# A two-layer mixer and expert step: one expert's up weights go to another place and are loaded before the scatters end, and a VectorE copy moves ahead of a register load

## The reference

```
def moe_ffn(h, w_router, b_router, w1, w3, w2):
    s = jax.nn.sigmoid((h @ w_router).astype(jnp.float32))
    sb = s + b_router.astype(jnp.float32)
    ...
    _, idx = lax.top_k(jnp.where(in_group, sb, NEG_INF), TOP_K)
    wsel = jnp.take_along_axis(s, idx, axis=-1)
    wsel = wsel / jnp.sum(wsel, axis=-1, keepdims=True)
    gates = ...
    hid = jax.nn.silu(jnp.einsum('bnd,edf->bnef', h, w1)) * jnp.einsum('bnd,edf->bnef', h, w3)
    return jnp.einsum('bnef,efd->bnd', hid * gates[..., None], w2).astype(h.dtype)
```

## Time and profile before

| what | value |
|---|---|
| median of 3 runs | 1187.36 us (1186.56 to 1190.74) |
| the profiled execution's own time | 1180.08 us |
| its span, first to last instruction | 1177.2 us |
| mean granted TensorE clock | 0.978 |
| busy share of the span: PE, PE weight loads, VectorE, ScalarE, GpSimd | 93%, 48%, 44%, 23%, 18% |
| chain that ended last: PE, DMA, VectorE, GpSimd | 74%, 11%, 5%, 4% |
| bytes moved by DMA | 288.29 MB, mean 245 GB/s |

### The profile page before, as it was taken

How to read it: one execution, slowest core, us unless ns; L and a number is a source line. 1 busy time by engine, 2 the same in 40 slices (tenths; PEclk the granted TensorE clock), 3 DMA queues, 4 the chain that set the end, 5 groups by cost and what they waited for, 6 DMA issues and landing times.

```text
span 1177.2 us, 14999 instructions
## 1 busy us (share of the span) xinstructions
PE 1094.7 (93%) x5084; PEld 569.2 (48%) x5084; DVE 522.6 (44%) x1291; ACT 275.8 (23%) x637; POOL 212.2 (18%) x297
## 2 busy tenths in 40 slices
PE   5999999899999799999899999989999988899985
PEld 3556766555444343345345576655544433234432
DVE  1133554776236542424351535478623563224236
ACT  2121121566011111111152112156601111111111
POOL 5027100101122310000363510010112231000022
PEclk9999899999999899999999999999999978999998
DMA  9587741795404899998565841179300489999834
GB/s 348 212 273 279 277 179 36 292 355 213 179 0 170 335 376 365 417 417 355 208 259 187 345 168 66 36 272 360 120 18 1 154 325 348 368 417 414 333 131 189
DMA packets 62842, 288.29 MB, mean 245 GB/s; under 512 B 9776, under 2 KB 10944, under 8 KB 46832
## 3 DMA queue, kind: packets, MB, share of 16 engines
q1 hardware_dynamic: 33344, 190.87, 42.4%
q0 software_dynamic: 22608, 77.70, 18.4%
q10 hardware_dynamic: 6816, 18.78, 4.2%
HBM read 237.96 MB, written 55.93 MB: 250 GB/s over the span
## 4 chain that ended last, share of the span: by engine, by line
PE 74%; DMA 11%; DVE 5%; POOL 4%; issue 3%; ACT 2%; SPq 1%; another core or an unknown queue 0%; ACTq 0%; POOLq 0%; DVEq 0%
PE ps L1797 14%; PE ps L1319 12%; PE ps L1620 12%; PE ps L1821 6%; DMA arena<-in_w 5%; PE ps L1554 3%; PE ps L1585 2%; PE ps L1254 2%; PE ps L1247 2%; PE ps L1565 2%; DMA bias_rows<-bias_tab 2%; PE ps L1855 1%; PE ps L1185 1%; DVE arena L2659 1%; PE ps L1230 1%
## 5 line engine op out<-in xcount | busy, mean ns | idle before, releaser
L1797 PE MATMUL ps<-arena 128*32 128x512 f32 (+1 forms) x1024 | 206.0, 616 | 10.5 <-DMA arena<-in_w 9.6
L1319 PE MATMUL ps<-arena 128*128 128x320 f32 x560 | 159.7, 439 | 2.9 <-DVE arena L2426 2.9
L1620 PE MATMUL ps<-arena 128*128 128x512 f32 x320 | 140.4, 594 | 2.4 <-issue 2.4
L1797 PEld LDWEIGHTS ps<-arena 128*32 128x32 f32 (+1 forms) x1024 | 74.7, 134 | 136.6 <-issue 135.1
L1319 PEld LDWEIGHTS ps<-arena 128*128 128x128 f32 x560 | 106.7, 193 | 47.0 <-DVE arena L2426 3.1
L2924 DVE COPY arena<-ps 128x512 f32<-128x512 f32 x28 | 19.4, 691 | 193.4 <-PE ps L1761 193.4
L1821 PE MATMUL ps<-arena 128*32 128x512 f32 (+1 forms) x512 | 101.6, 595 | 3.3 <-issue 3.3
L1620 PEld LDWEIGHTS ps<-arena 128*128 128x128 f32 x320 | 59.5, 190 | 74.6 <-issue 74.6
L1131 POOL DMA_DIRECT2D arena<-expert_in x36 | 18.8, 521 | 262.5 <-issue 262.5
L1821 PEld LDWEIGHTS ps<-arena 128*32 128x32 f32 (+1 forms) x512 | 34.3, 129 | 50.6 <-issue 50.6
L2169 ACT ACTIVATE arena<-ps 128x256 f32<-128x256 f32 x28 | 10.7, 383 | 186.9 <-PE ps L1797 186.9
(11 more groups left out here) (349 smaller groups left out, 1570.8 us busy)
## 6 DMA issues: line engine op xcount, KB each, us to landing
arena<-in_w SPq DMA_DIRECT2D x96, 1024.0 KB, 17.4
arena<-in_w_ada SPq DMA_DIRECT2D x40, 1024.0 KB, 6.9
expert_in<-arena POOLq DMA_DIRECT2D x2, 8192.0 KB, 32.1
arena<-in_w_t SPq DMA_DIRECT2D x10, 1024.0 KB, 10.0
arena<-in_w_ada_c SPq DMA_DIRECT2D x8, 1024.0 KB, 13.2
arena<-in_w_out SPq DMA_DIRECT2D x8, 1024.0 KB, 7.4
arena<-mod_rows POOLq DMA_DIRECT2D x16, 512.0 KB, 11.4
arena<-in_w_n SPq DMA_DIRECT2D x8, 928.0 KB, 9.3
```

The lines of the kernel that those rows point to most:

```text
L1319: ins = mm(out[:, 0:HALF], lhs[:, k, :], rhs[:, k, :], start=(first and k == 0), stop=(last and k == 3), skip_group_check=True)
L1620: ins = mm(out[:, n * 512:(n + 1) * 512], yT[:, k, t * P:(t + 1) * P], w[k // 2][:, k % 2, n * 512:(n + 1) * 512], start=(k == 0), stop=(k ...
L1797: ins = mm(out[lo:lo + n, :], hsT[b][:, k, lo:lo + n], w[role][:, k, :], start=(k == 0), stop=(k == KD - 1), skip_group_check=True)
```

## The change

Four things change, in both layers.

1. Place 2's up weights (role 2 is the first in it) go to `at_y`, columns 0 to 4095, in place of `at_h + 2 * SLOT`. Place 2's down weights are cut in two pieces of 1024 columns, the last 1024 columns of `at_h` and the last 1024 of `at_y`; sizes and the count of DMAs stay.
2. SyncE issues the two DMAs of up 2 after `roles_ready` alone. The waits for `tokens0` and for the scatters come after them, ahead of up 5.
3. VectorE's copy of the upper half of `tokens0` comes ahead of `value_load(rounds_i)`.
4. Six VectorE instructions that find role and capacity of each token's choices and the last unit's gates move from ahead of the loop to `rows_of_round`, which lies behind the copy of unit 0's transposed tokens. Their products go to an own buffer `r_chosen`, and their waits use another semaphore.

```
-        up_at = [at_ring + SLOT, at_ring + 3 * SLOT, at_h + 2 * SLOT, at_h]
-        down_at = [at_ring, at_ring + 5 * SLOT, at_h + 4 * SLOT, at_up]
+        up_at = [at_ring + SLOT, at_ring + 3 * SLOT, at_y, at_h]
+        down_home = [view(at_ring, 2, D), view(at_ring + 5 * SLOT, 2, D), view(at_h + TL * D, 2, KD * N_TOK)[:, :, 0:D], view(at_up, 2, D)]
...
+        r_chosen = view(at_a + D, 2, TT, NE)
...
                     wait(sp, roles_ready.sem, roles_ready.at(l, 1))
-                    filled(sp, l, "tokens0")
-                    wait(sp, scattered.sem, scattered.at(l, 16 * 2 * TT))
...
-                        for load, role in WEIGHTS_ORDER:
+                        for n, (load, role) in enumerate(WEIGHTS_ORDER):
+                            if n == 1:
+                                filled(sp, l, "tokens0")
+                                wait(sp, scattered.sem, scattered.at(l, 16 * 2 * TT))
...
-                for of_expert, of_choice in ((r_role_row, r_role), (r_cap_of, r_cap)):
-                    link(V(r_t, r_sel, of_expert.unsqueeze(1).unsqueeze(1).broadcast_to((P, 2, TT, NE)), ALU.mult))
-                    link(dve.tensor_reduce(of_choice, r_t, AX.X, ALU.add))
                 if l + 1 < DEPTH:
                     modulation_rows(l, l + 1)
                     modulation_columns(l, l + 1)
                     gates_of_choices()
-                link(dve.scalar_tensor_tensor(out=r_gate2, in0=r_role, scalar=float((NE - 1) * P), in1=gates,
-                                              op0=ALU.is_equal, op1=ALU.mult))
-                link(V(r_gate, r_gate2[:, 0], r_gate2[:, 1], ALU.add))
...
                 def rows_of_round(turn):
+                    for n, (of_expert, of_choice) in enumerate(((r_role_row, r_role), (r_cap_of, r_cap))):
+                        V(r_chosen, r_sel, of_expert.unsqueeze(1).unsqueeze(1).broadcast_to((P, 2, TT, NE)), ALU.mult)\
+                            .then_inc(back_chain, 1)
+                        dve.wait_ge(back_chain, turn * 16 + (2 * n + 1))
+                        dve.tensor_reduce(of_choice, r_chosen, AX.X, ALU.add).then_inc(back_chain, 1)
+                        dve.wait_ge(back_chain, turn * 16 + (2 * n + 2))
...
                 dve.sem_inc(passed, 1)
+                dve.tensor_copy(hs[:, 0, 512:1024], filled(dve, l, "tokens0")[:, 512:1024]).then_inc(first_high.sem, 1)
                 n_rounds = dve.value_load(rounds_i[0:1, 0:1], min_val=1, max_val=5)
-                dve.tensor_copy(hs[:, 0, 512:1024], filled(dve, l, "tokens0")[:, 512:1024]).then_inc(first_high.sem, 1)
```

More of the change, by code:

```diff
@@ L35 @@
 CREDIT = 2
-DVE_CHAIN = 171
+DVE_CHAIN = 165
 ROUNDS = N_TOK // P
@@ L859, in load_down @@
                     wait(sp, dn_full, used_down)
-                    sp.dma_start(view(down_at[q], 2, D), A["w2"][bass.ds(l, 1), bass.ds(e, 1), :, :]
+                    sp.dma_start(down_home[q], A["w2"][bass.ds(l, 1), bass.ds(e, 1), :, :]
                                  .rearrange("a b (k p) n -> p (a b k) n", p=P)).then_inc(down_in[q][0], 16)
@@ L1812, in down @@
                     for role, _, _, _ in EXPERT_UNITS[u]:
-                        w[role] = view(down_at[loaded(down_in, turn, role, 16)], 2, D)
+                        w[role] = down_home[loaded(down_in, turn, role, 16)]
                     pe.wait_ge(hidT_ready, base + u + 1)
@@ L2947, in rows_of_round @@
                 def rows_of_round(turn):
+                    for n, (of_expert, of_choice) in enumerate(((r_role_row, r_role), (r_cap_of, r_cap))):
[4 more added lines that the diff above has]
+                        dve.wait_ge(back_chain, turn * 16 + (2 * n + 2))
+                    dve.scalar_tensor_tensor(out=r_gate2, in0=r_role, scalar=float((NE - 1) * P), in1=gates,
+                                             op0=ALU.is_equal, op1=ALU.mult).then_inc(back_chain, 1)
+                    dve.wait_ge(back_chain, turn * 16 + 5)
+                    V(r_gate, r_gate2[:, 0], r_gate2[:, 1], ALU.add).then_inc(back_chain, 1)
                     role = r_role.rearrange("p a t -> p (a t)")
@@ L2954, in rows_of_round @@
                     dve.tensor_scalar(r_last, r_rel2, 1.0, None, ALU.add).then_inc(back_chain, 1)
-                    dve.wait_ge(back_chain, turn * 10 + 3)
+                    dve.wait_ge(back_chain, turn * 16 + 9)
                     dve.scalar_tensor_tensor(out=r_in, in0=r_rel, scalar=0.0, in1=r_in,
@@ L2959, in rows_of_round @@
                                              op0=ALU.is_equal, op1=ALU.mult).then_inc(back_chain, 1)
-                    dve.wait_ge(back_chain, turn * 10 + 5)
+                    dve.wait_ge(back_chain, turn * 16 + 11)
                     dve.scalar_tensor_tensor(out=r_in, in0=role, scalar=float((NE - 1) * P), in1=r_in,
@@ L2963, in rows_of_round @@
                     V(r_high, r_last[:, 0], r_last[:, 1], ALU.max).then_inc(back_chain, 1)
-                    dve.wait_ge(back_chain, turn * 10 + 7)
+                    dve.wait_ge(back_chain, turn * 16 + 13)
                     dve.scalar_tensor_tensor(out=r_at_row, in0=r_at_row, scalar=spare_row, in1=r_in,
@@ L2968, in rows_of_round @@
                     dve.tensor_scalar(r_high, r_high, 1.0, None, ALU.subtract).then_inc(back_chain, 1)
-                    dve.wait_ge(back_chain, turn * 10 + 10)
+                    dve.wait_ge(back_chain, turn * 16 + 16)
                     dve.tensor_scalar(back_i[:, :], r_at_row, spare_row, None, ALU.add).then_inc(back_ready, 1)
```

## The result

The median of 20 runs went from 1186.66 to 1173.24 us, ratio 0.9894, 95% interval [0.9873, 0.9915]: 1.06% faster, some 12.6 us (the two medians alone differ by a little more, 13.4 us; the ratio is not their quotient). The forecast was 1186.0 us with a range of 1181.5 to 1190.5 and a chance of 0.14 on faster.

What follows compares the result with a forecast made beforehand. The prediction took DMA engines to pace up to 85 us of each layer. Layer 0's +0.2 and layer 1's -1.6 us summed to -1.4 us, from 1187.36 to 1186.0 us, range 1181.5 to 1190.5.

Steps and rivals of the forecast that it cites:

- What bounds the kernel: Each layer: DMA engines pace up to 85 us; their idle time behind the scatters caps the win at 7.8 us, 0.66%.
- g: Time won at the gap behind the scatters: 1.2 us in layer 0, 1.6 in layer 1, lower bound 0.55 each.
- the clock: TensorE at unit 5: layer 0 newly pays 1.75 us for a lowered clock; layer 1 pays before and after.
- I let 0.7 us pass to the first byte (my choice): Early up 2 load: its first byte moves 0.7 us after issue, with 1.58 and 1.18 MB of scatters still to write.
- The scatters end last, 2.1 MB / 0.415 = 5.0 us later than before: Both layers: scatters share the engines with up 2's 2.1 MB and end near 406.0 and 966.5 us.
- The rule of sharing: DMA engines alternate between queues by whole packets; weights' packets are about twice as large, so up 2 takes 7.4 us.
- Layer 0 changes by +1.37 - g: Start of unit 7 in layer 0: 489.23 - g against 487.86 us, so +0.2 us.
- Unit 1's rows: Ahead of unit 1: layer 0's 3.59 us wait nearly goes, layer 1 gets a new 2.7 us one; neither moves the end.
- VectorE: Layer 1: unit 0 starts some 2 us sooner, worth nothing; layer 0: 1.1 us later, hidden by a wait.
- second rival: Both layers: scatters keep pace beside up 2, layer 0's clock does not fall; 7.8 us less, 1179.6 us; chance 0.14.

Runs made afterwards that it cites:

- the early load: Kernel before with the change's new places and SyncE's order (up 2 issued at `roles_ready`), VectorE as before, in both layers: 1172.49 us, ratio 0.9915.
- The filler: Kernel before with 16 useless 128x128 matmuls on TensorE ahead of its wait for unit 5's weights: 1184.1 us, ratio 0.9979.

## Why the prediction was wrong, step by step

**What bounds the kernel** held: in every trace the waits sit where TensorE runs into a DMA-paced stretch. The bound "7.8 us, 0.66%, at the very most" fell: 9 to 13 us were measured in the runs with the early load in both layers. DMA idle time is not all that the load could win; see g and the clock below.

**The step that failed first is "I let 0.7 us pass to the first byte (my choice)"**, and with it "The scatters end last, 2.1 MB / 0.415 = 5.0 us later than before". The first packet took 2.7 to 4.1 us; 0.7 us was too little even for idle engines (1.0 us and more). By the prediction 1.18 MB of scatters were still to be written in layer 1 when up 2 began to move; in the traces it was 0.1 to 0.2 MB, in layer 0 0.8 and 0.7 MB where up 2 was issued at 15.0 us, and 0.1 MB where it was issued at 17. All that follows from sharing, the scatters' end 5.0 us later and g = 0.55 us as the lower bound, was reckoned for a meeting that hardly takes place in layer 1 and takes place in two of four executions in layer 0. The scatters' end moved by 2.0 us in layer 1 and 3.2 in layer 0, in layer 1 only through the tail, which a reckoning in bytes does not see. The rule of sharing itself was right (124 packets beside 126). Where the scatters did end 3.5 us late or more, unit 5 came 1.4 us (layer 0) and 2.6 us (layer 1) sooner than the means without early load, near my 1.2 and 1.6.

**g.** I took 1.6 us in layer 1; unit 5 came 5.7 us sooner there (means 87.9 and 82.2), against 3.8 for the whole gap as I had reckoned it. From the first scatter to unit 5 the DMA engines moved 31.2 MB at 354 GB/s in the four layers without early load and 30.6 MB at 372 in the four with it. The share rose from 0.98 to 1.01, some 2.8 us: this is the gap. 0.6 MB less of other traffic had been moved by then, some 1.5 us, and the rest, some 1.4 us, is a higher rate at the same share, for which I have no cause. (The pair of traces shown above is an extreme one: 31.8 MB at 357 and 30.7 MB at 375.) The sentence that the last weight lands earlier "only by as much as the DMA engines stand idle less before it" thus fell too: it takes the other traffic ahead of unit 5's weights as fixed, an assumption that was not stated. In layer 0 unit 5 came 2.5 us sooner (87.7 and 85.2), where I had 1.2.

**The clock.** "Layer 0 changes by +1.37 - g" rested on one execution in which the wait at unit 5 was 1.10 us. In the three other executions with the old layer 0 it was over 7 us, with the lowered clock already paid; so there the change has nothing to add. In layer 1 I wrote that unit 5 "pays for the clock before and after". In three of four traces with the early load it no longer did: its waits there were 0, 0.57 and 3.21 us, its product took 7.05 to 7.07 us, and from unit 5 to unit 7 it took 23.3 to 23.4 us in place of 25.1 to 26.3. On average from unit 5 to unit 7 this is 1.8 us of layer 1's 7.5; in layer 0 it is a gain of 0.2 us, where I had charged 1.75. The filler shows the same from the other side. TensorE itself was not sooner at unit 2; but it did not stand idle there any more, and ran unit 2 in 7.07 us instead of 9.70 (8.42 and 8.77 in the other three).

**Unit 1's rows**: a new wait of 2.4 to 3.4 us in layer 1, as written (2.7), and it moves nothing in the traces that wait for weights later; where none follows (the early load in layer 1 only), it is the last thing for which TensorE waits there. **VectorE** was worth nothing that can be told, as written. The **second rival**, "the gap is filled", is nearest to what happens; it was given 0.14 and 7.8 us. Its mechanism holds in part: the scatters kept their pace only in some executions, and layer 0's product at unit 5 did run slowly in three of four with the early load, as it had in three of four without it.

What stays open is why 1 MB early gives as much as 2 MB, why the scatters' end moves by 0.2 us in one execution and 3.5 in another, and what makes the executions of one kernel differ by 17 us in the changed kernel. A part of the latter can be seen: the first scatter lies anywhere from 374.8 to 379.4 us in these traces, and a late one was followed by a short layer 0 (108.9 and 106.7 us); but the earliest, 374.75 us in the run with half of up 2, has a short one as well (108.2), and I tried nothing on it.

## What to carry to other kernels

Where a DMA-paced stretch begins with a wait for a semaphore, look at how long the DMA engines are idle around that wait, and put one transfer that doesn't need the wait into it: 1 MB issued ahead was enough here, worth 1% in the end. Ask when its first bytes will move, not when it is issued. Moving near the end of the other queue it costs little: in the traces up 2 issued at about 17 us had unit 7 start at 104.9 to 110.1, in layer 0 issued at 15.0 us at 111.2 and 112.7. And 2 MB that nobody needed, issued 1.4 to 3.6 us sooner than up 2 in the early load, cost 10.7 us, about their full length in both layers. And take a second execution before a term rests on the size of one wait: 1.10 us was 7 us in three of four.

## What the runs showed of the hardware

- A load issued from SyncE while GpSimd's indirect DMAs have the engines fully busy begins its first packet 2.7 to 4.1 us after its issue; behind the scatters' end it was 1.0 us with nothing else moving and 1.4 to 2.3 us otherwise. I had not expected that a queue of its own would have to wait so long.
- From then on both queues get the same number of packets (124 and 126 in 3.5 us), with 8 KB rows against 4 KB ones 69% and 32% of the time.
- The sharing also stretches a queue's tail: the scatters' last 4 KB packets, which started 0.16 us apart when alone, started 0.46 us apart beside the weights, and their end came up to 3.5 us later with 0.2 MB left.
- Behind a wait for weights, a part of the product that follows can run at the lower of TensorE's two levels: it took 7.05 to 7.08 us behind every wait up to 2.03 us, and 8.8 to 10.0 us behind every wait of 3.97 us and more (9.88 us at a granted clock of 0.71). In between both were seen: 8.77 us behind 2.15, 2.33, 3.29 and 3.79 us, 8.42 behind 3.04 and, with the filler ahead, 3.14, and 7.07 or 7.08 behind 2.82, 3.14, 3.21, 3.35 and 3.94. So the length of the wait alone does not tell what it costs.
